# Strassen's scheme for ten of the eleven down products of a feed-forward layer

## What is computed

```python
def _convffn(h, buf, w_up, conv_w, w_down):          # h: (tokens, 1024) after RMSNorm
    a = jnp.einsum('bld,df->blf', h, w_up)           # w_up: 1024 x 5632 (2 x D_FF, D_FF = 2816)
    a, buf_new = _causal_dwconv(a, buf, conv_w)      # three taps along the tokens, per column
    gate, up = jnp.split(a, 2, axis=-1)
    return jnp.einsum('blf,fd->bld', jax.nn.silu(gate) * up, w_down), buf_new   # w_down: 2816 x 1024
x = x + f                                            # f: what _convffn returns
```

## Time and profile before

| | |
|---|---|
| three executions | 3447.86, 3453.91, 3458.95 us (median 3453.91) |
| profiled execution | 3453.28 us, span of its instructions 3451.5 us |
| TensorE products / weight loads busy | 3243.1 us (94%) / 3039.6 us (88%) |
| VectorE, ScalarE, GpSimd busy | 2001.9 (58%), 902.0 (26%), 887.2 (26%) |
| products of up tiles and other inputs by `h_split`, 384 columns | 3 x 3072 |
| products of down tiles by `ffn_act`, 384 columns | 3 x 1056 |
| feed-forward stages | some 880 to 1735 and 2577 to 3426 us |

### The profile page before, as it was taken

The page is one execution under the profiler, slowest core; times in us unless marked ns, Lnnn a source line. Parts: engine busy times, 40 slices in busy tenths (PEclk is TensorE's granted clock), DMA queues, the critical chain, the costliest instruction groups (busy, mean ns, idle before and its releaser), DMA issues. The chain is left out here.

```text
span 3451.5 us, 56818 instructions
## 1 busy us (share of the span) xinstructions
PE 3243.1 (94%) x23942; PEld 3039.6 (88%) x23942; DVE 2001.9 (58%) x3541; ACT 902.0 (26%) x1655; POOL 887.2 (26%) x782
## 2 busy tenths in 40 slices
PE   7999997889999999999988999979899999999997
PEld 5988975779999999999988898648799999999996
DVE  6396564562655565555666855546537655555556
ACT  3244244243211111111233431532332111111112
POOL 3221110223322222222342212011243222222223
PEclk9999998799999999999999999979999999999998
DMA  5633231101111111111164322320011111111111
GB/s 189 193 95 109 85 111 59 67 18 43 42 40 41 43 43 37 44 43 43 36 185 145 100 77 87 112 102 9 29 42 43 43 37 44 43 43 43 37 43 66
DMA packets 123430, 234.13 MB, mean 68 GB/s; under 512 B 34020, under 2 KB 84452, under 8 KB 119848
## 3 DMA queue, kind: packets, MB, share of 16 engines
q1 hardware_dynamic: 121096, 227.35, 20.3%
q10 hardware_dynamic: 2080, 3.15, 0.3%
HBM read 173.54 MB, written 54.43 MB: 66 GB/s over the span
## 5 line engine op out<-in xcount | busy, mean ns | idle before, releaser
L268 PE MATMUL PS<-h_split,w_split 128*128 128x384 f32 x3072 | 1062.4, 346 | 21.9 <-PEq L205 9.8
L270 PE MATMUL PS<-h_split,w_split 128*128 128x384 f32 x3072 | 1041.0, 339 | 0.0
L269 PE MATMUL PS<-h_split,w_split 128*128 128x384 f32 x3072 | 1037.2, 338 | 0.0
L263 POOL TENSOR_TENSOR w_split<-w_full,w_split 128x1024 fp32r<-128x1024 f32 (+1 forms) x192 | 466.1, 2428 | 911.8 <-ACT w_split L255 911.8
L268 PEld LDWEIGHTS PS<-h_split,w_split 128*128 128x128 f32 x3072 | 583.6, 190 | 41.4 <-issue 16.3
L269 PEld LDWEIGHTS PS<-h_split,w_split 128*128 128x128 f32 x3072 | 580.6, 189 | 2.5
L270 PEld LDWEIGHTS PS<-h_split,w_split 128*128 128x128 f32 x3072 | 580.2, 189 | 0.0
L255 ACT CAST w_split<-w_full 128x1024 fp32r<-128x1024 f32 (+1 forms) x194 | 202.0, 1053 | 1307.9 <-PE PS L270 1167.8
L2380 DVE TENSOR_TENSOR x<-x,PS 128x384 f32<-128x384 f32 x528 | 285.4, 551 | 160.2 <-PE PS L270 158.5
L268 PE MATMUL PS<-ffn_act,w_split 128*128 128x384 f32 x1056 | 366.1, 347 | 2.1 <-DVE w_split L2387 1.1
L269 PE MATMUL PS<-ffn_act,w_split 128*128 128x384 f32 x1056 | 356.0, 337 | 0.0
(11 more groups left out here) (398 smaller groups left out, 4912.2 us busy)
## 6 DMA issues: line engine op xcount, KB each, us to landing
w_full<-in_w_up SPq DMA_DIRECT2D x88, 512.0 KB, 3.2
w_full<-in_w_down SPq DMA_DIRECT2D x44, 512.0 KB, 3.2
w_full<-in_w_in SPq DMA_DIRECT2D x40, 512.0 KB, 3.9
kq_keep<-split_rows SPq DMA_DIRECT2D x128, 128.0 KB, 2.4
kq_row<-kq_keep SPq DMA_DIRECT2D x32, 512.0 KB, 4.4
x<-x_keep SPq DMA_DIRECT2D x2, 4608.0 KB, 16.9
w_full<-in_w_out SPq DMA_DIRECT2D x16, 512.0 KB, 3.3
gdn_y<-y_keep SPq DMA_DIRECT2D x2, 3456.0 KB, 11.1
```

Source lines behind the costliest of these rows:

```text
L263: pool.tensor_tensor(ws[:, n % SSLOTS, 1, 0:w], wf[:, n % WSLOTS, 0:w], ws[:, n % SSLOTS, 0, 0:w].bitcast(F32), ALU.subtract).then_inc(w_l ...
L268: pe.matmul(out, w_hi, a_hi, start=first, stop=False)
L269: pe.matmul(out, w_hi, a_lo, start=False, stop=False)
L270: return pe.matmul(out, w_lo, a_hi, start=False, stop=last)
```

## The change

The first ten of the eleven down steps of a layer are computed by the Strassen-Winograd scheme. A step is a product of two by two blocks: the contraction is split into its two D_FF tiles, four rows `m` are split into two pairs, and the 1152 tokens into two halves of 576. A step is done as two mixes, `h` = 0 and 1, each for four of the eight rows. Seven block products replace eight; each is 2 (`p`, the rows of a pair) x 2 (288 columns each) x 3 products, so a mix has 14 `STEPS` of 6 products of 288 columns. A step's result lies in two banks; the three places are banks 4 and 5, 6 and 7, 2 and 3, the last shared with the up tiles' units.

- **Sums of weights** (`weight_sums`): GpSimd makes four sums of 256 columns, ScalarE casts in three pieces (256, 512, 1024 columns), GpSimd subtracts in three pieces.
- **Sums of activations**: VectorE makes T1 (`sums_early`, after the first product of a cycle), T3, T2 and T4 (`sums_late`, after the second). ScalarE casts and VectorE subtracts in `highs_early`/`lows_early` (two blocks each) and `highs_late`/`lows_late` (two blocks, then three). `highs_early` also makes two plain copies.
- **Results**: VectorE adds ten times 576 columns to `x` per mix (`mix_adds`). Four times a mix ScalarE copies a partial sum to `kept_sum` (`keep_sums`; TensorE goes on accumulating in that bank after it), and GpSimd adds it to `x` (`add_sums`).
- **Order**: up, up, mix 0, up, mix 1, up in cycles 1 to 9; after the last up tile both mixes of the tenth step, and then the plain down tiles of the eleventh.
- **Weight places**: two are left for feed-forward tiles (`slot_of`; a mix's seven blocks take more room), so tile n+1 is prepared while tile n runs, once tile n-1 has been multiplied (`slot_free`). The last plain tile waits for the second mix, and its low part is GpSimd's.
- VectorE's stream is now written out per cycle; only in the last pair of mixes do pieces of other work (`ending`) follow the additions, one each.

The core of the diff, without what the text above tells or what is only removed:

```diff
 def ffn_tiles():
...
+tiles = []
+for q in range(parts):
+    mixes = [("mix", q - 1, h) for h in range(2)] if q >= 1 else []
+    for i in range(4):
+        tiles.append(("up", 4 * q + i, (i % 2) * FF_TILES + 2 * q + i // 2))
+        if mixes and i in (1, 2):
+            tiles.append(mixes[i - 1])
+last = parts - 1
+tiles = [t for t in tiles if t[0] != "mix" or t[1] < last - 1]
+tiles += [("mix", last - 1, h) for h in range(2)]
+tiles += [("down", last, 2 * last + e) for e in range(2)]
+return tiles, 4 * parts
...
+if kind == "mix":
+    return d["w_down"][l, 2 * q:2 * q + 2, :, 512 * t:512 * t + 512].rearrange("e p c -> p e c"), KD * P
...
+def slot_of(n):
+    return n % SSLOTS if n < FFN_W else 2 * ((n - FFN_W + 1) % 2)
...
+A11, A12, A22, S1, S2, S3, S4 = range(7)
+B11, T1, B21, B22, T3, T2, T4 = range(7)
+MIXED = {"m1": (A11, B11), "m2": (A12, B21), "m3": (S4, B22), "m4": (A22, T4), "m5": (S1, T1),
+         "m6": (S2, T2), "m7": (S3, T3)}
+STEPS = (("m1", 0, 0), ("m5", 0, 1), ("m1", 1, 2), ("m6", 0, 0), ("m3", 0, 1), ("m6", 1, 2), ("m7", 0, 0),
+         ("m2", 0, 1), ("m7", 1, 2), ("m4", 0, 0), ("m5", 1, 1), ("m4", 1, 2), ("m2", 1, 0), ("m3", 1, 1))
+SUM_STEPS = (1, 3, 4, 6)
+ADD_STEPS = (2, 5, 7, 8, 9, 10, 11, 12, 13, 14)
+M_STEPS, M_ADDS, M_SUMS = len(STEPS), len(ADD_STEPS), len(SUM_STEPS)
+BANKS = (4, 6, 2)
...
+def x_part(h, p, i, j):
+    return x[:, 4 * h + 2 * i + p, HALF * j:HALF * (j + 1)]
...
+def slot_free(eng, n):
+    if n < 2:
+        return
+    kind, c, t = tiles[n - 2]
+    if kind == "up":
+        eng.wait_ge(upr, NB * (c + 1))
+    else:
+        eng.wait_ge(dnr, M_STEPS * (2 * c + t + 1))
...
+act.wait_ge(wsm, 2 * tiles[n][1] + tiles[n][2] + 1)
+act.copy(w[0][:, A11], raw[:, 0])
+act.copy(w[0][:, A12:A22 + 1], raw[:, 2:4])
+act.copy(w[0][:, S1:S4 + 1], w[2][:, S1:S4 + 1]).then_inc(w_hid, 1)
...
+def weight_sums(pool, link, n):
+    slot_free(pool, n)
+    pool.wait_ge(w_loaded[(FFN_W + n) % WSLOTS], 16 * ((FFN_W + n) // WSLOTS))
+    w, raw = mix_weights(n)[2], wf[:, (FFN_W + n) % WSLOTS, 0:KD * P].rearrange("p (i c) -> p i c", c=256)
+    link(pool.tensor_tensor(w[:, S1], raw[:, 1], raw[:, 3], ALU.add))
+    pool.tensor_tensor(w[:, S3], raw[:, 0], raw[:, 1], ALU.subtract)
+    link(pool.tensor_tensor(w[:, S2], w[:, S1], raw[:, 0], ALU.subtract))
+    pool.tensor_tensor(w[:, S4], raw[:, 2], w[:, S2], ALU.subtract).then_inc(wsm, 1)
...
+    return
+w, raw = mix_weights(n), wf[:, (FFN_W + n) % WSLOTS, 0:KD * P].rearrange("p (i c) -> p i c", c=256)
+pool.wait_ge(w_hid, FFN_W + n + 1)
+pool.tensor_tensor(w[1][:, A11], raw[:, 0], w[0][:, A11].bitcast(F32), ALU.subtract)
+pool.tensor_tensor(w[1][:, A12:A22 + 1], raw[:, 2:4], w[0][:, A12:A22 + 1].bitcast(F32), ALU.subtract)
+pool.tensor_tensor(w[1][:, S1:S4 + 1], w[2][:, S1:S4 + 1], w[0][:, S1:S4 + 1].bitcast(F32),
+                   ALU.subtract).then_inc(w_lod, 1)
...
             pe.matmul(PS[:, 4 + b, 0:BLK], ones[:, :], ss[:, b, :], start=True,
                       stop=True).then_inc(smr, 1)
+elif kind == "mix":
+    k = 2 * c + t
+    w = mix_weights(n)
+    pe.wait_ge(w_lod, FFN_W + n + 1)
+    pe.wait_ge(alo, 2 * (c + 1))
+    units = NB * (1 + max(m[1] for m in tiles[:n] if m[0] == "up"))
+    for i, (name, p, s) in enumerate(STEPS):
+        if i == 2:
+            pe.wait_ge(upf, 1 + max(u for u in range(units) if u % 4 in (2, 3)))
+        if i < 3 and k >= 1:
+            pe.wait_ge(added, M_ADDS * (k - 1) + (9, 10, 8)[i])
+        if name == "m6":
+            pe.wait_ge(skp, M_SUMS * k + 1 + p)
+        elif name == "m7":
+            pe.wait_ge(skp, M_SUMS * k + 3 + p)
+        elif i >= 3:
+            last_use = max(j for j in range(i) if STEPS[j][2] == s)
+            pe.wait_ge(added, M_ADDS * k + ADD_STEPS.index(last_use + 1) + 1)
+        a, b = MIXED[name]
+        fresh = name in ("m1", "m2", "m5")
+        for j in range(2):
+            out = PS[:, BANKS[s] + j, 0:HALF // 2]
+            cols = slice(HALF // 2 * j, HALF // 2 * (j + 1))
...
+def add_sums(q, h):
+    k = 2 * q + h
+    for i in range(M_SUMS):
+        p, j = i % 2, i // 2
+        pool.wait_ge(skp, M_SUMS * k + i + 1)
+        if i == 2:
+            pool.wait_ge(added, M_ADDS * k + 2)
+        xs = x_part(h, p, 0, j)
+        pool.tensor_tensor(xs, xs, kept_sum[(M_SUMS * k + i) % 3][:, :], ALU.add).then_inc(sad, 1)
...
+behind = tiles[n + 1:n + 2] if n >= 1 and kind != "down" else []
+for next_kind, *_ in behind:
+    if next_kind == "mix":
+        weight_sums(pool, link, n + 1)
+if kind == "mix":
+    add_sums(c, t)
+for _ in behind:
...
+lo(pool, n + 1)
...
 pool.tensor_copy(sample_view(row, FFN_TAPS, 0, pad),
...
+def highs_late(act, q):
+    act.wait_ge(afl, 2 * q + 2)
+    act.copy(a7[:, 0, B21:B22 + 1], halves(au[:, 0:TOK])).then_inc(ahi, 1)
+    act.wait_ge(asm, 2 * q + 2)
+    act.copy(a7[:, 0, T3:T4 + 1], a7f[:, T3:T4 + 1]).then_inc(ahi, 1)
...
+def keep_sums(act, q, h):
+    k = 2 * q + h
+    for i, step in enumerate(SUM_STEPS):
+        n = M_SUMS * k + i
+        act.wait_ge(dnr, M_STEPS * k + step)
+        if n >= 3:
+            act.wait_ge(sad, n - 2)
+        act.copy(halves(kept_sum[n % 3][:, :]), mixed_out(STEPS[step - 1][2])).then_inc(skp, 1)
...
+ending = kind == "mix" and c == LAST - 1
+if ending and t == 0:
+    highs_plain(act, 0)
+elif 1 <= n < len(tiles) - 2:
+    hi(act, n + 1)
+if kind == "mix":
+    keep_sums(act, c, t)
+if ending:
+    hi(act, n + 1 if t == 0 else n + 2)
+    if t == 0:
+        highs_plain(act, 1)
+if kind == "up":
+    q, j = divmod(c, 4)
+    if j == 0 and q >= 1:
+        highs_late(act, q - 1)
+    if j == 3 and q < LAST:
...
...
+def sums_late(q):
+    dve.wait_ge(afl, 2 * q + 2)
+    dve.wait_ge(ahi, 4 * q + 2)
+    dve.tensor_tensor(a7f[:, T3], au[:, HALF:TOK], a7f[:, T3], ALU.subtract)
+    link(dve.tensor_tensor(a7f[:, T2], au[:, HALF:TOK], a7f[:, T2], ALU.subtract))
+    dve.tensor_tensor(a7f[:, T4], au[:, 0:HALF], a7f[:, T2], ALU.subtract).then_inc(asm, 1)
+def lows_late(q):
+    dve.wait_ge(ahi, 4 * q + 4)
+    dve.tensor_tensor(a7[:, 1, B21:B22 + 1], halves(au[:, 0:TOK]), a7[:, 0, B21:B22 + 1].bitcast(F32),
+                      ALU.subtract)
+    dve.tensor_tensor(a7[:, 1, T3:T4 + 1], a7f[:, T3:T4 + 1], a7[:, 0, T3:T4 + 1].bitcast(F32),
+                      ALU.subtract).then_inc(alo, 1)
...
+def mix_adds(q, h, between=iter(())):
+    k = 2 * q + h
+    for i, step in enumerate(ADD_STEPS):
...
+dve.tensor_tensor(xs, xs, mixed_out(s), ALU.add).then_inc(added, 1)
+next(between, None)
...
+for q in range(LAST + 1):
...
+    convolve_tile(c - 1)
+    product(2 * q - 1)
+    sums_late(q - 1)
+    take(c, range(NB - 1))
+    lows_late(q - 1)
+    take(c, range(NB - 1, NB))
+convolve_tile(c)
+take(c + 1)
+if 1 <= q < LAST:
+    mix_adds(q - 1, 0)
+convolve_tile(c + 1)
+product(2 * q)
+take(c + 2)
+if 1 <= q < LAST:
...
+def ending():
+    low_plain(0)
+    yield True
+    yield from convolve(ups - 1, tiles[[t[:2] for t in tiles].index(("up", ups - 1))][2])
+    product(2 * LAST + 1)
+    yield True
+    yield True
+    yield True
+    yield True
+    low_plain(1)
+    yield True
+left = ending()
+for h in range(2):
+    mix_adds(LAST - 1, h, left)
+assert next(left, None) is None
+for u in range(KD * NB):
```

More of the change, by code:

```diff
@@ L89, in ffn_tiles @@
     parts = FF_TILES // 2
-    tiles, ups = [], 0
-    for q in range(parts + 1):
-        downs = [("down", q - 1, 2 * q - 2), ("down", q - 1, 2 * q - 1)] if q >= 1 else []
-        for i in range(4 if q < parts else 0):
-            if i == 3 and q < parts - 1:
-                tiles += downs
-            tiles.append(("up", ups, (i % 2) * FF_TILES + 2 * q + i // 2))
-            ups += 1
-        if q >= parts - 1:
-            tiles += downs
-    return tiles, ups
+    tiles = []
[10 more added lines that the diff above has]
+    return tiles, 4 * parts
 def build(nc, d):
@@ L2167, in _ @@
                                     pe.wait_ge(upf, u - 3)
+                                if after is not None and u % 4 in (2, 3):
+                                    pe.wait_ge(added, M_ADDS * after + 8)
                                 cols = slice(b * BLK, (b + 1) * BLK)
@@ L2317, in invert, with take @@
                         dve.reciprocal(s, s).then_inc(rcd, 1)
-                    def take(c):
-                        for b in range(NB):
+                    def take(c, blocks=range(NB)):
+                        for b in blocks:
                             u = c * NB + b
@@ L2428, in _ @@
+                    for h in range(2):
+                        mix_adds(LAST - 1, h, left)
+                    assert next(left, None) is None
+                    for u in range(KD * NB):
+                        add(u)
+                        m, b = down_unit(u)
+                        if b == 1 and m == 5:
+                            invert_next(0)
+                        if b == 2:
+                            next_row(m)
                     if final:
```

239 lines of the change are left out of this document (133 added, 106 removed).

## The result

The changed kernel takes 3470.86 us (median of 6 runs, 3470.2 to 3476.64) where the kernel before takes 3455.6 beside it (3447.86 to 3458.95): ratio 1.0045, interval 1.0034 to 1.0056. The forecast was 3455. The time lies inside the outer range, 3420 to 3486, but outside the forecast's own, 3440 to 3468, and the granted clock shows 0.50 inside the feed-forward stage, which was the sign of the slower rival. The profiled execution took 3471.98 us for a span of 3469.8, 18.3 more than before.

The account below looks back on a forecast made before the run. TensorE, busy for 94% of the span, was taken to bound the kernel. 3453.28 - 13.7 (cycles) + 12.4 (layer ends) + 3 (clock there) = 3455 us; own range 3440 to 3468, outer range 3420 to 3486.

Parts of the forecast that it names:

- the slower rival: First mix of each cycle: the 2.9 us wait lets the clock fall, 36 us more, 3491 us; chance 0.19.
- Products: TensorE in the mixes: 288-column products follow each other at 0.132 us, saving 3.66 us a cycle, 66 us if nothing waits.
- The new wait: First mix of each cycle: TensorE waits 2.9 us for GpSimd's low parts, leaving 13.7 us gained over 18 cycles.
- The end of a layer: Last pair of mixes and last down tile: 6.2 us later a layer, 12.4 lost, plus 3 for the clock.
- if every second wait does it: First mixes of the cycles: the clock falls at only every second new wait, giving 3473 us.
- Faster: First mix of each cycle: wait only 1.0 us, 34 us less, 3421 us, or 3410 with a lighter end; chance 0.27.
- VectorE's pace in a mix: Additions in the mixes: 0.75 us per 0.79 us step tips over, 18 us more, 3473 us; chance 0.09.

Follow-up runs that it names:

- that run: Kernel with GpSimd's weight sums ahead of the state copies, plus the first mix starting on its first low parts: 3414.99 us, ratio 0.9883 against the kernel before.
- the last run: Kernel with sums ahead of copies and early mix start, plus 36 unread TensorE products ahead of the second of the two last mixes: 3408.02 us, ratio 0.9864.

## Why the prediction failed where it did

- **Products.** Pitch forecast 0.132, measured 0.1318. A load of 0.19 us overlaps here too: the rule of the Trainium skill (TensorE: Matmul & The Clock Gate, Part 3, "What overlaps and what doesn't") by which a load overlaps running products only when the row group differs is not seen with 288 columns either. With no wait a cycle is 73.15 (72.8 forecast; between 1000 and 1600 us the waits view lists nothing for the weight loads of that run): 3.3 us of work saved, 3.66 forecast.
- **The new wait.** Forecast 2.9, 18 times; measured 2.8, 18 times. The chain is right link by link: counted from the start of the cycle (1168.3, two up tiles or 25.3 us before their end) the sums begin at 17.3 us (17.1 forecast) and end at 21.7 (21.7), the low parts end at 28.0 (28.2). A cycle with the clock up is 75.83 (75.7 forecast): the gain is 11.0, not 13.7.
- **The step that failed: "the slower rival".** I put a wait of 2.9 us between one gap that left the clock up and one that did not the earlier trace rows, gave the fall 0.19, and left it out of the sum. It fell after 7 of 18, 1.51 us each, 10.6 us; I had priced one fall at 2. That busy products remove it and that gaps of 1.6 us or less never showed it was measured. The two rows were poor neighbours: the gap of 3.40 us stands among small products where the clock had been at 0.50 shortly before (594.8 to 601.6), in no stretch as full as this one. My "if every second wait does it" is 3473, close to what came, but in part by luck: it adds 18 us for the falls where 10.6 came, and the rest came from the other terms.
- **The end of a layer.** The second mix starts at 20.65 (20.7 forecast), and with the clock up its last load is at 31.8 (31.8 forecast), as the last run shows. With the clock's fall that is 34.3 and 33.5 instead of the 31.8 + 1.5 assumed, the first mix starts 0.3 late, not 0.6, and the last low part is 0.8 later (0.9 forecast). 16.5 us lost, 15.4 forecast. The start at 20.65 is right in part by luck: the first mix is through sooner than I had it (last load at 15.3; I freed its last step at 16.2), and two late pieces on VectorE take 2.3 and 2.4 us beside GpSimd's low parts (the second takes 0.28 alone), so that TensorE is idle for 5.2 us at once and not for 3.6.
- **The sum.** Forecast against measured: cycles -13.7 against -11.0, clock in the cycles 0 against +10.6, ends +15.4 against +16.5: these three are 14.4 of the 16.6 us that the span came out above the forecast.
- **Rivals.** Faster: excluded, the turns on GpSimd are there. VectorE's pace in a mix: 0.75 of 0.79 held; between 1000 and 1600 us the waits view lists no wait for an addition.

Open: why 7 of 18 equal gaps let the clock fall. It is 7 in each of the four profiles with the wait of 2.8 us, every second or third cycle, so it isn't chance alone; no run here separates what decides it. Open too: how the end of a layer splits between VectorE and GpSimd once one of them has less to do; the runs show only that the other is next.

## What to carry to other kernels

Less work on the busiest engine is a gain only while every chain that feeds it is shorter than the work that covers it: walk the queues in order and find the last instruction ahead of each start, as moving four sums ahead of two copies was worth 1.5% here. A gap costs more than its length when the clock falls behind it (1.51 us each time here), so price a new wait of some 3 us with its clock. And look first at whether the consumer really needs all it waits for: letting the first step start on the first part gave as much as reordering two queues.
